# Convolution FFNs: one 512-column matmul for the high weight part times both token parts, with the two PSUM halves summed by VectorE

## The reference

```python
def conv_ffn(u, w_up, conv_w, conv_b, w_down):      # u: 256 x 1024, w_up: 1024 x 5632, w_down: 2816 x 1024
    hdn = causal_dwconv(u @ w_up, conv_w) + conv_b  # 3 taps along the tokens, per channel
    gate, val = jnp.split(hdn, 2, axis=-1)
    return (jax.nn.silu(gate) * val) @ w_down
```

## Time and profile before

| | |
|---|---|
| time of three runs | 1234.59, 1237.45, 1238.65 us (median 1237.45) |
| span of the profiled execution, first to last instruction | 1232.7 us |
| PE busy in it | 1215.1 us, 99% |
| DVE, ACT, POOL busy | 847.2, 682.4, 53.0 us |
| mean granted TensorE clock | 0.998 of full |
| the two convolution FFNs, gate/up of group 1 to the end of the last down | about 176 us each |

### The profile page before, as it was taken

One profiled execution on the slowest core, in us unless ns is written; L12 is line 12 of the kernel. 1 busy time (PEld: TensorE's weight loads), 2 busy tenths in 40 slices (PEclk: granted clock), 3 DMA queues, 4 the chain that ended last, 5 costly groups with the idle time before them and its releaser, 6 DMA issues. The chain is left out here.

```text
span 1232.7 us, 19105 instructions
## 1 busy us (share of the span) xinstructions
PE 1215.1 (99%) x7351; PEld 1069.0 (87%) x7351; DVE 847.2 (69%) x1153; ACT 682.4 (55%) x1009; POOL 53.0 (4%) x84
## 2 busy tenths in 40 slices
PE   8999999999999999999999999999999999999998
PEld 6888888887888888889898799999899887999997
DVE  5555457778654446757966776776868988766666
ACT  5444446464544435656635765555775657655455
POOL 0400000010000000101400000000000000000000
PEclk9999999999999999999999999999999999999999
DMA  9965555425645555544322665555553335555620
GB/s 336 272 221 175 174 205 175 138 69 171 212 173 174 183 204 205 174 157 138 134 69 87 205 205 192 176 172 177 204 205 100 107 100 209 178 185 184 204 103 35
DMA packets 139206, 209.10 MB, mean 170 GB/s; under 512 B 9949, under 2 KB 101235, under 8 KB 139137
## 3 DMA queue, kind: packets, MB, share of 16 engines
q1 hardware_dynamic: 136256, 199.39, 48.1%
q0 software_dynamic: 2864, 8.76, 2.5%
q10 hardware_dynamic: 16, 0.00, 0.0%
HBM read 207.08 MB, written 1.05 MB: 169 GB/s over the span
## 5 line engine op out<-in xcount | busy, mean ns | idle before, releaser
L303 DVE TENSOR_TENSOR wlo<-raw,whi 128x1024 fp32r<-128x1024 f32 x374 | 440.6, 1221 | 45.1 <-ACT whi L298 43.3
L298 ACT ACTIVATE whi<-raw 128x1024 fp32r<-128x1024 f32 x374 | 374.1, 1050 | 42.4 <-PE psum L331 40.4
L329 PE MATMUL psum<-whi,xh 128*128 128x512 f32 (+1 forms) x688 | 275.3, 400 | 4.8 <-DVE wlo L303 3.5
L331 PE MATMUL psum<-whi,xl 128*128 128x512 f32 (+1 forms) x688 | 267.4, 389 | 0.0
L330 PE MATMUL psum<-wlo,xh 128*128 128x512 f32 (+1 forms) x688 | 266.8, 388 | 0.0
L329 PE MATMUL psum<-xh,whi 128*128 128x256 f32 x928 | 263.5, 284 | 0.0
L330 PE MATMUL psum<-xl,whi 128*128 128x256 f32 x928 | 262.6, 283 | 0.0
L331 PE MATMUL psum<-xh,wlo 128*128 128x256 f32 x928 | 262.6, 283 | 0.0
L329 PEld LDWEIGHTS psum<-xh,whi 128*128 128x128 f32 x928 | 177.9, 192 | 0.9
L330 PEld LDWEIGHTS psum<-xl,whi 128*128 128x128 f32 x928 | 178.0, 192 | 0.7
L331 PEld LDWEIGHTS psum<-xh,wlo 128*128 128x128 f32 x928 | 178.0, 192 | 0.0
(11 more groups left out here) (373 smaller groups left out, 1184.5 us busy)
## 6 DMA issues: line engine op xcount, KB each, us to landing
raw<-in_ffn_w_up SPq DMA_DIRECT2D x131, 512.0 KB, 5.2
raw<-in_ffn_w_down SPq DMA_DIRECT2D x88, 512.0 KB, 4.4
raw<-in_ffn_w_gate SPq DMA_DIRECT2D x43, 512.0 KB, 4.6
raw<-in_c_w_in SPq DMA_DIRECT2D x32, 512.0 KB, 4.7
raw<-in_ab_w_in SPq DMA_DIRECT2D x28, 512.0 KB, 4.7
raw<-in_w_in SPq DMA_DIRECT2D x18, 512.0 KB, 4.5
raw<-in_w_out SPq DMA_DIRECT2D x8, 512.0 KB, 4.1
raw<-in_ple_w_gate SPq DMA_DIRECT2D x8, 512.0 KB, 5.0
```

The lines of the kernel that those rows point to most:

```text
L298: nc.scalar.activation(hi, r, ACT.Copy).then_inc(hi_done, 1)
L303: nc.vector.tensor_tensor(lo, r, hi.bitcast(F32), ALU.subtract).then_inc(lo_done, 1)
L329: nc.tensor.matmul(pe_out, sh, mh, start=start, stop=False, skip_group_check=True)
L331: return nc.tensor.matmul(pe_out, sl, mh, start=False, stop=stop, skip_group_check=True)
```

## The change

- The two token parts become halves of one tile `x2`, so that for a chunk of channels `x2[:, :, kc, :]` is 512 moving columns in two runs of 256: the high part and the low part.
- For groups 1 to 10 of ffn2 and ffn3, `three` with three 256-column matmuls becomes `both_tokens` with two: the high weights by all 512 columns of `x2`, into a whole PSUM bank, and the low weights by the 256 columns of `xh`, into the first half of the bank. Each block (j, c) of a group now has its own bank, 4 + 2j + c, and all groups use the same four banks.
- The result is the sum of the two halves of a bank. For each j VectorE copies the second halves to SBUF (`both`) and adds the first halves to them (`dve_sum`): two instructions of 128 x 512 for each j. The middle tap, the bias and the shifted taps now read `both` instead of PSUM.
- TensorE goes through a piece with j outermost. Behind the last gate matmul of a group it raises `gate_done`, on which the first copy waits. Before it writes the gate banks and the value banks of the next group it waits for `summed` of the group before. Its wait for `hid_lo` of two groups earlier is gone.
- Group 0 is turned into banks 2 and 3 instead of 4 and 5.

The SwiGLU layers ffn0 and ffn1 keep `three`. The diff, cut to its core:

```diff
-        xh = sb("xh", [P, KC, SEQ], F32R)
-        xl = sb("xl", [P, KC, SEQ], F32R)
+        x2 = sb("x2", [P, 2, KC, SEQ], F32R)
+        xh, xl = x2[:, 0, :, :], x2[:, 1, :, :]
...
+        def both_tokens(j, c, wh, wl, kc):
+            nc.tensor.matmul(bank(4 + 2 * j + c), wh, x2[:, :, kc, :], start=(kc == 0), stop=False, skip_group_check=True)
+            return nc.tensor.matmul(bank(4 + 2 * j + c, 0, SEQ), wl, xh[:, kc, :], start=False, stop=(kc == KC - 1),
+                                    skip_group_check=True)
...
-        def gate_or_up(n, q, j, c):
-            return psum[:, 4 + 2 * q + j, 256 * c:256 * c + 256]
+        both = arena[:, 6144:7168].rearrange("p (j c t) -> p j c t", j=2, c=2)
+        def first_columns_of(j, c):
+            return psum[:, 2 + j, 256 * c:256 * c + 256]
+        def sums_of(n, g):
+            return 20 * (n - 2) + 2 * (g - 1)
...
 
-            if not isinstance(g, int) or n * GROUPS + g >= 2:
+            if n < 2 and (not isinstance(g, int) or n * GROUPS + g >= 2):
                 pe.wait_ge(hid_lo, g + n * GROUPS - 1)
             for k in range(4):
                 if isinstance(g, int) and g == 0 and k % 2 == 0:
                     wait_turned(pe, f"ffn{n}", k // 2)
                 pe.wait_ge(lo_done, p + k + 1 + 2 * RING * i)
                 wh, wl = weights(p + k, 2, 512)
-                for kk in range(2):
+                for kk in range(2 if n < 2 else 0):
                     kc = 2 * k + kk
-                    if n < 2:
-                        for t in range(NT):
-                            tok = slice(t * P, t * P + P)
-                            last = three(bank(4 + 2 * q + t), xh[:, kc, tok], xl[:, kc, tok], wh[:, kk, :], wl[:, kk, :],
-                                         start=(kc == 0), stop=(kc == KC - 1))
-                        continue
-                    for c in range(2):
-                        for j in range(2):
+                    for t in range(NT):
+                        tok = slice(t * P, t * P + P)
+                        last = three(bank(4 + 2 * q + t), xh[:, kc, tok], xl[:, kc, tok], wh[:, kk, :], wl[:, kk, :],
+                                     start=(kc == 0), stop=(kc == KC - 1))
+                for j in range(0 if n < 2 else 2):
+                    if k == 0 and not (isinstance(g, int) and g == 1 and n == 2):
+                        pe.wait_ge(summed, sums_of(n, g - 1) + (j + 1 if not (isinstance(g, int) and g == 1) else 0))
+                    for kk in range(2):
+                        for c in range(2):
                             col = slice(256 * j + 128 * c, 256 * j + 128 * c + 128)
-                            last = three(gate_or_up(n, q, j, c), wh[:, kk, col],
-                                         wl[:, kk, col], xh[:, kc, :], xl[:, kc, :],
-                                         start=(kc == 0 and c == 0), stop=(kc == KC - 1))
+                            last = both_tokens(j, c, wh[:, kk, col], wl[:, kk, col], 2 * k + kk)
+                    if k == 3 and j == 0:
+                        last.then_inc(gate_done, 1)
                 last.then_inc(used, 1)
                 if k in after_piece:
                     after_piece[k]()
...
                 nc.scalar.activation(sg[:, q], psum[:, 4 + 2 * q:6 + 2 * q, 0:256], ACT.Silu).then_inc(sg_ready, 1)
                 return
             for j in range(2):
+                if not first:
+                    act.wait_ge(summed, sums_of(n, g) + j + 1)
                 for c in range(2):
                     f = g * 2 + (FC * j + c)
-                    last = nc.scalar.activation(cg[:, q, j, c, :], gate_or_up(n, q, j, c),
+                    last = nc.scalar.activation(cg[:, q, j, c, :], first_columns_of(j, c) if first else both[:, j, c, :],
                                                 ACT.Identity, scale=tap(n, 2, f), bias=tap(n, 3, f))
                 last.then_inc(conv_mid, 1)
             if last_piece is not None:
...
 
-        def dve_hidden(dve, n, g, q, i):
+        def dve_sum(dve, n, g, j, p, i):
+
+            if j == 0:
+                dve.wait_ge(gate_done, g + 10 * (n - 2))
+            else:
+                dve.wait_ge(used, p + 2 * RING * i - 2)
+            nc.vector.tensor_copy(both[:, j], psum[:, 4 + 2 * j:6 + 2 * j, SEQ:2 * SEQ]).then_inc(second_out, 1)
+            dve.wait_ge(second_out, sums_of(n, g) + j + 1)
+            nc.vector.tensor_tensor(both[:, j], psum[:, 4 + 2 * j:6 + 2 * j, 0:SEQ], both[:, j], ALU.add)\
+                .then_inc(summed, 1)
+
+        def dve_hidden(dve, n, g, q, p, i):
             G0 = n * GROUPS
             if n < 2:
                 dve.wait_ge(sg_ready, g + G0 + 1)
...
+            first = isinstance(g, int) and g == 0
+            for j in range(0 if first else 2):
+                dve_sum(dve, n, g, j, p, i)
...
                         y = cg[:, q, j, c, lag:SEQ]
                         last = nc.vector.scalar_tensor_tensor(
-                            y, gate_or_up(n, q, j, c)[:, 0:SEQ - lag], tap(n, k, g * 2 + (FC * j + c)), y,
+                            y, (first_columns_of(j, c) if first else both[:, j, c, :])[:, 0:SEQ - lag], tap(n, k, g * 2 + (FC * j + c)), y,
                             ALU.mult, ALU.add)
                     last.then_inc(done, 1)
```

15 lines of the change are left out of this document (9 added, 6 removed).

## The result

| | before | after |
|---|---|---|
| median of 22 runs of each, taken together | 1234.58 us | 1236.93 us |
| lowest, highest | 1233.83, 1238.65 | 1235.47, 1240.13 |
| ratio, with its 95% interval | | 1.0015 (1.0008 to 1.0022) |
| span of the profiled execution | 1232.7 | 1233.9 |
| from the last turned tile of group 0 to the last down matmul: ffn2, ffn3 | 172.22, 172.23 | 172.73, 172.86 |

The change makes the kernel 1.0 to 2.7 us slower, by 1.9 at the middle of the interval. The interval leaves out 1, so the loss is there, but it is under the 0.3% that the prediction set as its bound. The forecast was a gain of 2.5 us, a ratio of 0.998.

What follows compares the result with a forecast made beforehand. TensorE, busy 99% of the span, was taken to bound the kernel. Saving 8.5 us in matmuls and adding 6.0 us of waits gave -2.5 us: 1237.45 to 1235.0 us, range for 8 in 10 1230.0 to 1242.0.

Steps and rivals of the forecast that it cites:

- 640 x 0.0133 = 8.5 us: Gate/up on TensorE: 640 steps each drop one matmul's fixed 13 ns, a step going from 0.360 to 0.3467 us.
- bound of 0.355: Upper bound for a gate/up step: 0.235 for the 512 plus 0.120 for the 256, saving 3.2 us.
- lower bound of 0.3367: Lower bound for a gate/up step: 0.2267 plus 0.11, rounded to 0.340, saving 12.8 us.
- Rival 3: Gate/up: each change of width costs, 0.02 in every step, making it 0.367 us; +8.1 us, 1245.5 us; chance 0.14.
- Rival 4: Gate/up: the 13 ns is not each matmul's cost; step 0.355 to 0.359, 1239.6 to 1242.2 us; chance 0.13.
- deciding point: Step of 0.357 us from which width changes decide: saving 1.9, waits 5.5, sum +3.6 us.
- first down product: Start of each FFN: TensorE comes 0.43 us earlier, the low split only 0.11, so it waits 0.15 us.
- third piece of group 2: Each FFN: VectorE's low split is ready at 729.0, TensorE there at 728.6; with a restart 0.45 us.
- border of groups 9 and 10: Tail of each FFN: with no down product between, TensorE waits 0.4 us for group 9's sums.
- hidden block of group 10: Tail of each FFN: `hidl` ready at T10 + 10.1, needed at T10 + 8.19; with a restart 2.0 us.
- Rival 2: Tail waits are covered because VectorE gets to the sums sooner; 2.1 us of waits in all, 1231 us; chance 0.12.
- carried difference of 4.8 us: Whole kernel: median of runs stood 4.8 us above the profiled span, added to turn span 1230.2 into 1235.0 us.

Runs made afterwards that it cites:

- the kernel with three small matmuls: Kernel after with each 512-column matmul split back into two of 256, keeping new banks, sums and waits: 1240.22 us, ratio 1.0043 to before.
- the variant by banks: Kernel after with each block's low matmul placed behind the next block's high one, so high to low always changes bank: 1237.48 us, one run.
- the runs of four: Kernel after with four blocks' 512-column matmuls first, then their four 256-column ones: 1234.11 us, ratio 0.9992 to before.
- the runs of eight: Kernel after with four high, four low matmuls, alternate halves starting with the width the last ended on: 1233.49 us, ratio 0.9989 to before.
- the run of all three together: Kernel after with longer runs of one width, group 9's last products moved ahead, and second-half copies on ScalarE: 1229.87 us, ratio 0.9959 to before.

## Why the prediction was wrong

**The step that failed is the term "640 x 0.0133 = 8.5 us".** It took the start difference of a long run of each width as the price of one matmul, and added the two: 0.3467. Measured is 0.3533. That is 0.0067 saved a step, 640 x 0.0067 = 4.3 us, half of the term. In gate/up of a group it is 11.51 - 11.29 = 0.22 us and not 0.43. The bound of 0.355 held, the choice inside the bounds didn't. That was the pace of nine steps in ten; the others did go at 0.3467, so the sum was no impossible price, only not the usual one. I took the rows at a change of width to add up "to about that too". They add up to 0.34, and the lower bound of 0.3367 was rounded up to 0.340; neither supports 0.3467. And I set aside that the first six 512s behind a run of 256s take 0.23 us rather than 0.2267. Every 512 of the changed kernel is such a first one. The row was there, and rivals 3 and 4 both named it.

**By mechanism.** Rival 3, "each change of width costs", comes nearest, as longer runs of one width did bring time back. But it had 0.02 a step where 0.0067 was measured, on the near side of its own deciding point, 0.357. And it is not shown as the mechanism: in group 10 the width changes just as often, and the change costs nothing against the long-run paces. Rival 4's effect, little saved, came true in part. The trace doesn't carry its cause in the form given: in long runs both widths keep their 13 ns, in before and in every experiment. The page rule beside it (the Trainium skill, TensorE: Matmul & The Clock Gate, Back-to-back issue gap) would have had 1.6 us saved. The section gives that formula for isolated matmuls and says that it leaves out the weight load, which each matmul has here. The rows show 4.3, between it and the forecast.

**The sum, mended.** Forecast -2.5. The step adds 8.5 - 4.3 = +4.2. The down product, which I had left at its price, is 0.035 longer in each group (5.503 against 5.468, from the fine starts): 20 x 0.035 = +0.7. The waits came to 2.7 us an FFN instead of 3.0: -0.6. Together +1.8, where the runs give +1.9 and the FFN windows +1.1. Of the 0.7 between, 68 x 0.0067 = 0.5 are the steps that went at 0.3467. With the forecast's waits alone the sign turns at a step of 0.351 us: 640 x (0.360 - 0.351) = 5.8.

**The waits were right, one by one.** All four appeared. A fifth of 0.2 us, not forecast, came behind ffn2, and the stretch there is no longer for it. With their restarts:

| wait in each FFN | forecast, us | measured in ffn3 |
|---|---|---|
| first down product | 0.15 | 0.14 |
| third piece of group 2 | 0.45 | 0.20 |
| border of groups 9 and 10 | 0.4 | 0.43 |
| hidden block of group 10 | 2.0 | 1.91 |

The third piece came in shorter because TensorE arrived later: 16 steps of 0.3533 instead of 0.3467 are 0.1 us, and the down product ahead of it has its 0.035. The count of the tail held within 0.15 us all the way: the sums start at T10 + 1.63 (1.7 forecast), the taps at T10 + 4.27 (4.35), `hidl` is ready at T10 + 9.94 (10.1), with T10 = 1210.16. At the border the copy starts at T9 - 1.2 (-1.19) and the addition is done at T9 + 0.2 (+0.23). That the largest wait fits so well is luck in part: the count put group 10 at 0.3467 a step, and it is one of the groups that went at that. At 0.3533 TensorE would have come 0.2 us later and waited the less, as with the operand in one run. Rival 2 had these waits covered, and falls: they are there in full. That they are real time is shown by the kernel with three small matmuls: at the old pace it is 4.05 us longer over the two windows. The other order of the last products shows the same for ffn3: six matmuls in the gap, 1.4 us off the window and none of it back.

**What was costed at nothing** held. The sums in the loop cost nothing (its group with three small matmuls is 16.98 us, as before). So does the single set of banks, shown by the same run, and so does the operand in two runs. That the wait for `hid_lo` and the transfers cost nothing wasn't tried by themselves, but nothing in that same group of 16.98 leaves room for them.

**The chances.** The step of 0.3533 lay between the forecast's own range (within 2 ns of 0.3467) and rival 4 (from 0.355 on), with no case for it. A half-way case deserved the weight I gave to the forecast. The point that the carried difference of 4.8 us came from a median of three runs, which 22 runs put 2.9 us lower, is a second error. It has the other sign, and hides most of the first in the absolute time.

**What stays open.** Why a 512 behind 256s is slower in most steps and not in all. Against 32 x 0.3467 = 11.09 us, gate/up of a group takes 0.20 more with 32 changes to 256 and back, 0.20 again with the 24 of the variant by banks, 0.11 with the 8 of the runs of four, and 0.06 with the 5 of the runs of eight (three of its high runs are of eight, two of four). Per change these are 6, 8, 13 and 11 ns, and none in group 10 of after. So it is no fixed amount per change. Longer runs bring the time back, and that is shown by the two variants; that the change of width is what costs it is not. Behind a wait the same instructions can fall into the faster pace and stay in it until the down product, which points to where each matmul falls against the ones before it, and no run tests that. The experiments exclude the operand's layout, and the bank as far as it was varied. A step with equal widths (a 512 for the low halves too) wasn't tried, as it adds columns.

## What to carry to other kernels

The pace of a long run of one kind of instruction is not the price of one of them in a mixture: look for the rows at which the kind changes, and take their price if the change makes every instruction such a one. Where a new instruction order is free, keep like widths together: by order alone the same matmuls saved 640 x 0.0115 = 7.4 us in runs of eight, against 4.3 one by one, both by the pace in the loop; the two windows are 2.5 us shorter. A wait at the end of a stage, where the buffers and the covering work run out, can eat a gain that the loop really has; look there for independent work to move into the gap, and for a way to make the late engine faster. The two are not worth the same: work moved into the gap kept its gain where nothing hung on the end of the stage (ffn3), and gave it back where the next stage waited for the same late result (ffn2); an earlier result kept it in both. So read the stretch behind the stage too.

## What the runs showed of the hardware that was not expected

- Matmuls with 128-column weight loads and moving operands of 256 and 512 columns in turn take 0.3533 us for the pair at 2.4 GHz in nine pairs of ten, where runs of each take 0.120 and 0.2267. The others, behind some waits, take 0.3467, the sum of the two, with the same instructions and clock. The pair takes 0.350 in runs of four and 0.3485 in runs of four and eight.
- A moving operand in two runs of 1 KB, 8 KB apart, streams as fast as one in one run (11.29 us for 32 pairs either way). With the neighbours that write to the same PSUM bank halved, from four in eight to two, it is 11.29 again.
- After a wait of 1.8 us the second matmul comes 0.34 us behind the first instead of 0.23; after 0.4 us, 0.31 to 0.33. A short wait of TensorE costs some 0.08 to 0.11 us beyond its length.
- The granted clock of TensorE was 1.00 (2.4 GHz) in the windows of the FFNs, but it was not so throughout. From 10 to 14 us it was 0.62 in before and 0.60 in after, behind 4 us in which TensorE was busy for 1.8. It fell later and for longer, to 0.66 and 0.50 from 14 to 22 us in the run with the last products reordered, and not at all in the run of all three together. Its lower level is 1.2 GHz. Of the 52 runs of before beside the experiments, the eight with a mean granted clock of 0.996 or less took 1237.1 us or more, and the other 44 at most 1236.8.
- So time ahead of the FFNs scatters by more than the whole change is worth: the window of ffn2 starts at 708.5 to 712.8 us in ten profiled executions, in kernels that hardly differ there. TensorE's wait for the first inputs, 0.36 to 3.3 us, is part of it but no measure of it: the run of all three has 1.3 us of it and starts ffn2 earliest. A ratio of few runs can't see a microsecond through this; a window over the stage can, if the stretch behind it is read as well.
